# Awaited results on VectorE, fused gated one-hot rows, and the order of rows and experts, in a one-core decoder layer

## The reference, cut to what matters

```python
s = einsum("bhcd,hckd->bhck", q, peer_keys)            # 8 heads, 2 halves, 128 keys
sv, si = top_k(s, 16)
cand = sv[:, :, 0, :, None] + sv[:, :, 1, None, :]     # sums of the two halves
fv, fi = top_k(cand.reshape(..., 256), 16)
eidx = take_along_axis(si0 * 128 + si1, fi)            # 16 of 16384 experts a head
gate = softmax(fv)
act = gelu(einsum("bhkd,bd->bhk", peer_u[eidx], xb))
y = einsum("bhk,bhkd->bd", gate * act, peer_v[eidx])
```

## Time and profile before

| | |
|---|---|
| three timed runs | 4322.27, 4328.28, 4328.25 us, median 4328.25 |
| profiled execution, its own time | 4289.39 us |
| span of it, first to last instruction | 4287.2 us |
| TensorE busy, share of the span | 3754.9 us, 88% |
| VectorE | 3029.5 us, 71% |
| ScalarE | 970.3 us, 23% |
| GpSimd | 1817.6 us, 42% |
| moved by DMA | 1158.75 MB, mean 270 GB/s |
| mean granted clock of TensorE | 0.918 |

### The profile page before, as it was taken

How to read it: one execution, slowest core, us unless ns; L and a number is a source line. 1 busy time by engine, 2 the same in 40 slices (tenths; PEclk the granted TensorE clock), 3 DMA queues, 4 the chain that set the end, 5 groups by cost and what they waited for, 6 DMA issues and landing times. The chain is left out here.

```text
span 4287.2 us, 71337 instructions
## 1 busy us (share of the span) xinstructions
PE 3754.9 (88%) x28107; PEld 2509.6 (59%) x28107; DVE 3029.5 (71%) x5964; ACT 970.3 (23%) x2043; POOL 1817.6 (42%) x1489
## 2 busy tenths in 40 slices
PE   6996888899988987888888796669999999999998
PEld 5776775656655557787865455555445444455444
DVE  0373522589988864777756488868888888977777
ACT  1342210115432332232311015850000000010001
POOL 0015200064433412434335127735666666666665
PEclk8998889899999999898979897679999999999999
DMA  7353356498767756767679523469999999999998
GB/s 194 115 177 94 97 176 229 146 402 276 260 227 266 284 200 225 252 233 251 205 260 380 214 80 62 97 227 404 410 389 410 398 407 407 379 413 414 413 413 325
DMA packets 400417, 1158.75 MB, mean 270 GB/s; under 512 B 78470, under 2 KB 157387, under 8 KB 382507
## 3 DMA queue, kind: packets, MB, share of 16 engines
q0 software_dynamic: 207216, 687.87, 44.3%
q1 hardware_dynamic: 151124, 420.50, 26.4%
q10 hardware_dynamic: 41743, 45.82, 3.2%
HBM read 1047.82 MB, written 116.80 MB: 272 GB/s over the span
## 5 line engine op out<-in xcount | busy, mean ns | idle before, releaser
L2887 PE MATMUL x_vps<-l_c_v,x_w 128*128 128x512 f32 x1536 | 676.7, 601 | 33.8 <-DVE x_w L2936 33.8
L2879 PE MATMUL x_sps<-c_big,l_c_wo 128*128 128x384 f32 x2048 | 673.6, 491 | 26.9 <-DMA l_c_wo<-u_cols 23.8
L388 POOL DMA_INDIRECT l_w_ring<-u_rows,k_eidx x256 | 304.9, 1191 | 891.1 <-DVE l_w_dots L444 388.1
L388 POOL DMA_INDIRECT w_ring<-u_rows,k_eidx x384 | 480.7, 1252 | 406.6 <-DVE w_dots L444 230.2
L2879 PEld LDWEIGHTS x_sps<-c_big,l_c_wo 128*128 128x128 f32 x2048 | 391.7, 192 | 309.2 <-DMA l_c_wo<-u_cols 31.3
L461 DVE SCALAR_TENSOR_TENSOR l_c_share<-w_ring,w_wts,l_c_share 128x1024 f32<-128x1024 f32 x384 | 493.6, 1285 | 96.2 <-DMA w_ring<-v_rows,k_eidx 84.6
L2887 PEld LDWEIGHTS x_vps<-l_c_v,x_w 128*128 128x128 f32 x1536 | 295.7, 193 | 408.8 <-issue 361.3
L388 POOL DMA_INDIRECT w_ring<-v_rows,k_eidx x384 | 410.4, 1069 | 157.0 <-issue 109.6
L388 POOL DMA_INDIRECT l_w_ring<-v_rows,k_eidx x256 | 296.8, 1160 | 282.5 <-DVE l_w_yacc L461 219.4
L461 DVE SCALAR_TENSOR_TENSOR l_w_yacc<-l_w_ring,l_w_wts,l_w_yacc 128x1024 f32<-128x1024 f32 x256 | 328.9, 1285 | 24.8 <-DMA l_w_ring<-v_rows,k_eidx 16.3
L444 DVE CUSTOM_DVE_ANT_0 w_ring<-w_ring,w_h 128x1024 f32<-128x1024 f32 x256 | 302.5, 1222 | 37.5 <-DMA w_ring<-u_rows,k_eidx 35.8
(11 more groups left out here) (675 smaller groups left out, 6234.1 us busy)
## 6 DMA issues: line engine op xcount, KB each, us to landing
l_c_wo<-u_cols SPq DMA_DIRECT2D x64, 1024.0 KB, 8.6
l_c_v<-v_rows SPq DMA_DIRECT2D x32, 2048.0 KB
e_c_w<-w_tiles SPq DMA_DIRECT2D x54, 512.0 KB, 3.5
l_c_w<-w_tiles SPq DMA_DIRECT2D x51, 512.0 KB, 6.9
l_c_wo<-s_G SPq DMA_DIRECT2D x16, 1536.0 KB, 9.2
s_rw<-l_q_out SPq DMA_DIRECT2D x48, 384.0 KB, 5.3
s_G<-l_c_share ACTq DMA_DIRECT2D x8, 2048.0 KB, 8.5
l_c_kept<-s_rw SPq DMA_DIRECT2D x28, 384.0 KB, 7.6
```

The lines of the kernel that those rows point to most:

```text
L388: pool.indirect_dma_start(out=self.ring[:, r, :], out_offset=None, in_=self.A[table], in_offset=bass.IndirectOffsetOnAxis(ap=idx[:, s:s + ...
L2879: mm = pe.matmul(sps[n % 2][:, 0:ND * P], u[n % 4][:, k, :], hT[:, k, :], start=(k == 0), stop=(k == KT - 1))
L2887: mm = pe.matmul(vps[k][:, x * 512:(x + 1) * 512], w[:, e, k * P:(k + 1) * P], v[:, e, x * 512:(x + 1) * 512], start=(c == 0 and e == 0), ...
```

## The change

1. `Chooser` counts its operations and waits (`need`) only where an operation reads what an earlier one wrote. `best16` is reordered: the second index search of a row comes after the first operation of the next row, with two copies of the scratch row. The experts' numbers are made for both rank halves side by side, in two buffers. The trunk, the layer norms and the row additions lose their own waits in the same way.
2. In `scatter`, VectorE makes each of its two gated one-hot rows in one operation (compare and multiply), and ScalarE no longer scales them.
3. Dots and additions of a group alternate, on VectorE and in GpSimd's issue order.
4. `experts`: the product with `v` goes expert by expert, the three blocks inside; each half of `v` is loaded when its own tiles are read; three groups of rows lie in each half of a chunk; the first loads come in another order.
5. Seams: `merge` also writes the first mixed tile (`mT0`) to its place in the next stage, and loads the first input block and `w_out` at its last step (`w_out` was loaded at step 2); `fronts` no longer loads them. The last step of `merge` has no group of rows.

```diff
+    def put(self, ins):
         self.n += 1
         ins.then_inc(self.link, 1)
-        self.dve.wait_ge(self.link, self.n)
+        return self.n
+    def need(self, n):
+        if n > self.seen:
+            self.dve.wait_ge(self.link, n)
+            self.seen = n
...
+        V, copy = self.V, self.T[copy_at[0]][:, copy_at[1], :]
+        first = self.put(V.max(val[:, 0:8], src))
+        self.last8()
+        self.need(max(first, self.used.get(copy_at, 0)))
+        less = self.put(V.match_replace(copy, val[:, 0:8], src, LOW))
+        self.read = self.put(V.max_index(idx[:, 0:8], val[:, 0:8], src))
+        self.need(less)
+        self.open = (self.put(V.max(val[:, 8:16], copy)), copy_at, copy, val, idx)
...
     def add(self, dve, n):
...
+        if s:
+            dve.wait_ge(self.S["used"], self.v_at(n - 1) + 1)
         dve.wait_ge(self.got[q % self.RING], self.landed(q))
-        self.mark(dve, V.scalar_tensor_tensor(ya[:, :], self.ring[:, q % self.RING, :], self.wts[:, s:s + 1], ya[:, :], ALU.mult, ALU.add),
-                  self.S["used"], q + 1)
+        V.scalar_tensor_tensor(ya[:, :], self.ring[:, q % self.RING, :], self.wts[:, s:s + 1], ya[:, :], ALU.mult, ALU.add).then_inc(self.S["used"], 1)
...
-            if x < 4 and g < self.NGT:
-                self.dot(dve, 4 * g + x)
+            if x % 2 == 0 and g < self.NGT:
+                self.dot(dve, 4 * g + x // 2)
+            if x % 2 and 0 <= v < self.NGT:
+                self.add(dve, 4 * v + x // 2)
...
-                V.tensor_tensor(two[q % 2][:, 0:PER - BY_ACT, :], numbers[:, 0:PER - BY_ACT, :], wanted(1, q, PER - BY_ACT), ALU.is_equal).then_inc(S["one_done"], 1)
+                for t in range(PER - BY_ACT):
+                    c = PER * q + t
+                    ins = V.tensor_scalar(two[q % 2][:, t, :], T["iota"][:, 0:NKEY], byslot[:, 1, c:c + 1], byslot[:, 2, c:c + 1], ALU.is_equal, ALU.mult)
+                ins.then_inc(S["one_done"], 1)
...
-                act.wait_ge(S["one_done"], n + 1)
-                for t, c, to in tokens[0:PER - BY_ACT]:
-                    act.activation(to, to, ACT.Copy, scale=byslot[:, 2, c:c + 1])
...
-        before = lambda e: 1 if e % 2 and e // 2 < PERC else 0
-        behind = lambda k: len(range(CH // 2 + k, PERC, ND))
+        AMID = CH // 2 - 1
+        before = lambda e: 1 if e % 2 and e // 2 < min(PERC, AMID) else 0
+        behind = lambda k: len(range(AMID + k, PERC, ND))
...
+            def load_v(c, a):
+                sp.wait_ge(S["v_psum"], VQ * (c - 1) + a + 1)
+                sp.dma_start(v[:, QUAD * a:QUAD * (a + 1), :], A["v_quads"][VQ * c + a]).then_inc(v_in[a], 16)
...
             rows.load_h(sp, 0)
+            rows.load_scores(sp, 0, rows.later[0])
+            load_u(2)
             for j in range(2):
                 sp.wait_ge(g_out[j], G_STORES)
             load_g(0)
-            rows.begin(sp, 1)
+            rows.begin(sp, 1, 1)
+            load_u(3)
...
+                last = c == NCH - 1
+                order = [(k, e) for k in range(ND) for e in range(CH)] if last else [(k, e) for e in range(CH) for k in range(ND)]
...
-                if i == 2:
+                if i == KT - 1:
                     for k in range(KT):
                         sp.dma_start(A["sb_wo"][:, k, :], A["w_out"][k]).then_inc(wo_in, 16)
+                    sp.dma_start(h0[:, :], A["x_pad"][block0]).then_inc(h0_in, 16)
...
+                V.tensor_tensor(mT0[:, i, 0:cols0.stop - cols0.start], g[j][0][:, cols0], g[j][1][:, cols0], ALU.add)
...
-            load(0)
-            load_h(0)
```

More of the change, by code:

```diff
@@ L346, in begin @@
         f = self.later[0] if self.first is None else self.first
-        if f is not None and not self.begun:
+        if f is not None and not self.begun and not scored:
             self.load_scores(sp, 0, f)
@@ L467, in moments @@
         V, lnk = self.nc.vector, self.ch.lnk
-        for c in range(2):
-            lnk(V.bn_stats(st[0:rows, c, :], x[:, c * 512:(c + 1) * 512]))
+        self.ch.put(V.bn_stats(st[0:rows, 0, :], x[:, 0:512]))
+        lnk(V.bn_stats(st[0:rows, 1, :], x[:, 512:1024]))
         lnk(V.bn_aggr(ag, st[0:rows, :, :].rearrange("p a b -> p (a b)")))
@@ L1832, in _ @@
             sp.wait_ge(wo_in, 16 * KT)
+            sp.wait_ge(h0_in, 16)
             if pt.last:
@@ L1883, in _ @@
                                     ALU.mult).then_inc(gated[j][x], 1)
+                    bg.dve(dve, 4 * plan["group"](i))
+                for x in range(2):
                     dve.wait_ge(gated[j][x], r + 1)
-                    bg.dve(dve, 4 * plan["group"](i))
+                V.tensor_tensor(mT0[:, i, 0:cols0.stop - cols0.start], g[j][0][:, cols0], g[j][1][:, cols0], ALU.add)
                 if r:
@@ L2634, in choose @@
                 if x == 15:
+                    ch.need(ch.read)
                     dve.sem_inc(S["scs_read"], 1)
@@ L2760, in _ @@
                         ch.part(x)
+                    ch.last8()
+                    ch.need(ch.n)
             for k in range(NSC):
@@ L2843, in _ @@
                     load_g(c + 1)
+                for a in range(VQ if c + 1 < NCH else 0):
+                    load_v(c + 1, a)
                 for k in range(ND):
                     rows.sp(sp, behind(k))
-                if c + 1 < NCH:
-                    load_v(c + 1)
                 if c == NCH - 3:
@@ L2880, in _, with add @@
                     mm.then_inc(S["s_psum"], 1)
-                for k in range(ND):
-                    for e in range(CH):
+                def add(k, e):
+                    for x in range(2):
+                        mm = pe.matmul(vps[k][:, x * 512:(x + 1) * 512], w[:, e, k * P:(k + 1) * P], v[:, e, x * 512:(x + 1) * 512],
+                                       start=(c == 0 and e == 0), stop=(c == NCH - 1 and e == CH - 1))
+                    return mm
+                last = c == NCH - 1
+                order = [(k, e) for k in range(ND) for e in range(CH)] if last else [(k, e) for e in range(CH) for k in range(ND)]
+                for k, e in order:
+                    if k == 0:
                         pe.wait_ge(S["w_done"], CH * c + e + 1)
@@ L2885, in _ @@
                             pe.wait_ge(v_in[e // QUAD], 16 * c)
-                        for x in range(2):
-                            mm = pe.matmul(vps[k][:, x * 512:(x + 1) * 512], w[:, e, k * P:(k + 1) * P], v[:, e, x * 512:(x + 1) * 512],
-                                           start=(c == 0 and e == 0), stop=(c == NCH - 1 and e == CH - 1))
-                    mm.then_inc(S["v_psum"], 1)
+                    mm = add(k, e)
+                    if (e == CH - 1) if last else (k == ND - 1 and e % QUAD == QUAD - 1):
+                        mm.then_inc(S["v_psum"], 1)
         @block.scalar
@@ L3027, in program @@
         A["tiles"] = choice_tiles(lambda n, s, d=F32: held("k_" + n, s, d))
-        with ExitStack() as c4:
-            trunk(PARTS[0], none, nothing, c4)
+        with ExitStack() as c4, ExitStack() as c5:
+            trunk(PARTS[0], none, nothing, c4, c5)
             A["sb_v"] = c4.enter_context(nc.sbuf_tensor("e_c_v", [P, CH, DM], F32))
```

241 lines of the change are left out of this document (148 added, 93 removed).

## The result

The changed kernel took 4232.01 us (median of 4 runs, 4221.58 to 4234.73), the kernel before 4327.48 on the same chip: a ratio of 0.9777, 95% interval 0.9759 to 0.9796. The forecast was 4219. The profiled execution took 4221.58 us (span 4219.5) at a mean granted clock of 0.930.

The account below looks back on a forecast made before the run. TensorE leads the trunk, VectorE close behind; VectorE and ScalarE fill the scatter, TensorE and DMA the experts' stage. Savings 18 + 32 + 10 + 26 + 3 + 20 = 109 us bring 4328.25 to 4219 us, range 4160 to 4290.

Parts of the forecast that it names:

- The price of a wait: On VectorE, a wait removed where the next operation is ready saves 0.11 us; bounds 0.03 and 0.11.
- Rival (a): Waits on VectorE are nearly free, 0.03 us each: only 46 us saved in all, 4282 us; chance 0.13.
- Before the scatter: Selection stage: shorter selections on VectorE remove most of TensorE's 21.1 us gap, saving 18 us (bounds 5 and 21).
- The scatter: VectorE's turn falls from 2.78 to 2.31 us and ScalarE's to 2.33, saving 32 us (bounds 8 and 40).
- are worth something only as a pair: In the scatter, fused one-hot operations and missing waits pay only together, since VectorE's and ScalarE's turns are equally long.
- Rival (b): TensorE at a low clock becomes the scatter's bound, which gives 10 us instead of 32: 4241 us; chance 0.12.
- The step that failed: GpSimd's scattered additions, ending 57.6 us before the stage, start earlier too and do not yet bind at 50 us saved.
- Seams: Making or loading first tile and input in merge, w_out at its last step, saves 5 us each, 10 (bounds 0 and 41).
- Trunk: Late trunk: VectorE loses some 104 us of work and waits; a quarter reaches the path, 26 us (bounds 0 and 60).
- Experts: Experts' stage: expert-by-expert products, earlier loads and less VectorE work save 20 of 52 us above the DMA floor.
- (c): Gains carry through: half of the trunk's 104 us reaches the path and experts give 30: 4183 us; chance 0.17.
- (d): Slower: alternating dots and additions delay a group's last dot 3.9 us, ScalarE waits, costing 187 us: 4406; chance 0.05.

Follow-up runs that it names:

- run 10: The changed kernel measured again, unaltered, on one chip with the kernel before: 4182.34 us, ratio 0.9732 to the kernel before.
- run 9: The kernel before, unchanged, profiled again on the chip where the changed kernel was measured again: 4286.84 us.
- run 12: Changed kernel with the last 16 scattered additions moved into the experts' stage and one-hot rows unfused, scaled by ScalarE as before: 4194.16 us, ratio 0.9772.
- run 2: Changed kernel with every selection operation awaited at once again, new order and fused rows kept: 4260.11 us, ratio 0.9853.
- run 7: Changed kernel with the old one-hot rows (one comparison for two tokens, ScalarE scaling), VectorE's waits still removed: 4185.24 us, ratio 0.9739.
- run 3: Changed kernel with the last 32 of the third dense block's 128 scattered additions left out: 4193.96 us, ratio 0.9704.
- run 8: Changed kernel with the old seams: first mixed tile and input block loaded in the selection stage, w_out at merge's third step: 4198.39 us, ratio 0.9765.
- run 5: Changed kernel with VectorE's waits on its own results in the scan put back: 4197.61 us, ratio 0.9772.
- run 6: Changed kernel with the experts' stage in its old order of products, row groups and loads: 4173.72 us, ratio 0.9716.
- run 1: Changed kernel with row work in its old order, four dots then four additions, fetched in that order too: 4228.12 us, ratio 0.9792.

## Why the prediction was right, and where not

The sum of 109 us stands against 95.5 (first measurement) and 111 (run 10) by the timed runs, and 98.6 between the profiled executions of runs 9 and 10. By its terms, against the stages of runs 9 and 10:

- **The price of a wait** (0.11): 0.16 in the scatter's turn. Outside the scatter a row of five takes 1.17 us instead of 1.84, 0.13 for each. Right in kind and low in size; the overlap seen at the two long kinds of operation holds for MAX8, FIND_INDEX8 and MATCH_VALUE_LOAD. Rival (a) is out.
- **Before the scatter** (18): 22.7. TensorE's wait of 21.1 fell to 7.7. It passes the bound of 21.1: TensorE's busy time there fell as well, 178.81 to 174.35, at a mean granted clock of 0.91 instead of 0.86.
- **The scatter** (32): 36.4 of work, from the transposes to the last product. VectorE's turn, where nothing held it, came to 2.17 (2.31 foreseen: 0.51 for the fused pair, not 0.42, but 1.05 for the rest, not 1.28), ScalarE's to 2.32 (2.33 foreseen), as its timeline in run 10 shows; in the nine turns that follow, VectorE too starts only every 2.28:

```profile
2657.65 0.66 ACT L2601 ACTIVATE l_f_two<-k_iota,l_f_byslot 128x128 f32<-128x128 f32 x2
2658.34 0.88 ACT L2605 ACTIVATE l_f_two<-l_f_two,l_f_byslot 128x128 f32<-128x128 f32 x2
2659.13 1.04 ACT L2616 ACTIVATE l_c_share<-l_f_gps 128x512 f32<-128x512 f32 x1
2659.97 0.65 ACT L2601 ACTIVATE l_f_two<-k_iota,l_f_byslot 128x128 f32<-128x128 f32 x2
```

  That fused rows and missing waits "are worth something only as a pair" is half right. In the scatter the fused rows alone give 1 us, the missing waits alone 18, the fused rows on top of them 20. With the old rows ScalarE's turn stays at 2.74 us in run 12, as forecast, but the stage also has turns (sums, positions, experts' numbers) in which VectorE alone is late. Rival (b) did not come: the mean clock in the scatter went up, 0.70 to 0.75.
- **The step that failed:** "they start earlier by what the first selection saves ... so they are next, but not yet". GpSimd's additions ended last. Two things were wrong in it. They hardly started earlier: from the first mixing product it is 145.8 us before and 141.9 after. The first selection was done 17.5 us sooner, but the gates need ScalarE's Exp, which stands in ScalarE's queue behind the scores of another block, so the gain became a wait. First run 9, then run 10:

```profile
2539.84 0.29 DVE L238 TENSOR_REDUCE k_gs<-l_f_at_gate 128x8 f32<-128x128 f32 x1 [3.85 <-ACT l_f_at_gate L2513]
```

```profile
2483.12 0.29 DVE L274 TENSOR_REDUCE k_gs<-l_f_at_gate 128x8 f32<-128x128 f32 x1 [17.51 <-ACT l_f_at_gate L2586]
```

  And they take longer: 264.1 us from the first start to the last before, 286.6 after, with 12.5 and 24.8 us of waits for their own landing. The change itself does that, by the missing waits in the selection: with these put back it is 262.4 us (run 2), with the old one-hot rows and no waits 287.3 (run 7). The same operations of the experts' numbers show how. First run 10, where VectorE does not pause between them:

```profile
2531.33 0.99 DVE L249 TENSOR_TENSOR k_eq<-k_iota,k_fif 128x800 f32<-128x800 f32 x1
2531.47 3.59 POOL L2550 DMA_INDIRECT s_G<-l_f_at_gate,l_f_at_u  x1 [0.30 <-issue]
...
2535.36 3.58 POOL L2550 DMA_INDIRECT s_G<-l_f_at_gate,l_f_at_u  x1 [0.30 <-issue]
```

  and run 2, where each is awaited:

```profile
2599.26 1.56 POOL L2551 DMA_INDIRECT s_G<-l_f_at_gate,l_f_at_u  x1 [0.30 <-issue]
2600.64 0.99 DVE L250 TENSOR_TENSOR k_eq<-k_iota,k_fif 128x800 f32<-128x800 f32 x1
2601.12 1.94 POOL L2551 DMA_INDIRECT s_G<-l_f_at_gate,l_f_at_u  x1 [0.30 <-issue]
```

  More transfers do not explain it: the DMA engines are busy 0.33 of the time about the long additions (2527 to 2539 us of run 10) and 0.41 about the short ones (2596 to 2606 of run 2). The prediction had no term for what a VectorE without pauses does to GpSimd. By what path VectorE holds GpSimd up, and why three of the landing waits of run 10 are 5.4 to 5.8 us where run 9 has at most 2.3, no run shows. The hold is 30.4 us (33.7 from the last product of the scatter to the first of the experts, 3.3 before), and run 3 gave back 31: without it the terms before the scatter and of the scatter would have made 59, not the 50 of the forecast. As it is they made 28.7.
- **Seams** (10): 22 by run 8 against run 7, twelve late and ten early, though in the early part the stage behind gave some back (late project only 2.9 us earlier in run 10). The uncovered load of w_out did not come: the merge stage moved 334 GB/s instead of 310 and got shorter. The term looked at the wrong wait. TensorE's 20.4 us for the mixed tile only became 16.7 at the barrier, as the prediction's "most of the 20.4 ... stay" has it; 11 of the 12 late us are the wait for merge weights queued behind w_out (run 8), and in the move of w_out the prediction saw only a possible cost.
- **Trunk** (26) and early part (3): 33.9 for project, pairs and scan. The selection's share of the project is 8 us by run 2 (403.8 against 396), the scan's own waits 7 to 21 by run 5. A third of the 104 us forecast for VectorE reached the path, not a quarter. Early: the pairs take 147.3 to 150.3 us in all traces of the changed kernel and its variants against 153.4 and 154.4 before, and the early selection stage is 1 to 6 us longer; the early scan's scatter hides the rest.
- **Experts** (20): 17.0, with DMA at 402 GB/s against 398. The size is near, the reason is not: the order of the products and loads gave nothing (run 6). Which of VectorE's savings gave it stays open. Putting back the selection's waits (run 2), the additions' order and waits (run 1) or the order of products (run 6), one at a time, each left the stage between 1404 and 1412 us. No run put back two of them, so that any one could be enough, and this was not tried.
- **Rivals.** (c), the gains carry through, did not come: it wanted 52 us from the trunk and 30 from the experts, where 34 and 17 were measured. (d): its sign was there (TensorE waits 25.6 us for ScalarE's activation, ScalarE 885.0 for dots), by the new order of the experts' stage and not by the alternation, and it costs 4 to 9 us at most, not 187: a group has 14 us and ScalarE's part in it is short.

That the number came out near is partly luck, errors that cancel: against the forecast the selection before the scatter and the scatter's own work gave 9 us more, the trunk 8 and the merge stage 11; the early part gave 5 less, the experts 3 less, and GpSimd took 30.

## What to carry to other kernels

When several engines finish a stage within some tens of us of each other, a gain on one is worth only the distance to the next. Work out that next engine's end from its own chain (what starts it, on whose queue that stands, and how it slows when the engine beside it no longer pauses), not from its slack before. A fused operation and a removed wait can hide each other: build all four combinations before calling one worthless. And compare two traces stage by stage only if they are from one chip; an unedited stage that differs by 25 us is the sign that they are not.

## What the runs showed of the hardware

- One kernel's scan stage took 604.2 us on one chip and 560.3 on another, with more than twice as many idle times of TensorE that have no releaser (61 to 71 against 21 to 30, at products of 64 columns, some 12,600 in the stage). The other stages of the two traces agree within 5 us.
- An awaited short VectorE operation costs 0.13 to 0.16 us more than one that is not: a selection row of five is 1.84 us awaited and 1.17 not, and 1.05 where it stands between other work. A comparison and multiplication with two scalars per partition over 128 columns takes 0.25 us in a row of two.
- GpSimd issues a scattered addition of 128 single values in 1.56 us with 0.30 to the next. Beside VectorE operations of 320 and 800 columns that follow one another without a pause it took 3.58 and 3.59 us (run 10), beside the same operations with a wait after each 1.56 to 1.95 (run 2). In the traces with waits in the selection none is over 2.62 us, in those without them the longest is 3.59 to 4.53.
